# Second layer of a two-block network: three query columns side by side, and the memory written tile by tile behind them

## The reference, cut to what matters

```python
u = rms_norm(h, g_mix_pre[l])
u = sliding_window_sink_attention(u, positions, od_w_qkv[o], od_sinks[o], od_w_o[o])   # 16 heads, 4 kv heads
h = h + rms_norm(u, g_mix_post[l])
u = memory_cross_attention(rms_norm(h, g_x_pre[l]), mem, g_mem[l], w_xq[l], w_xkv[l], w_xo[l])
...
# inside memory_cross_attention: depends on mem alone, not on u
kv = (rms_norm(mem, g_mem) @ w_kv).reshape(B, M, 2, X_HEADS, X_HD)
```

## Time and profile before

| | us |
|---|---|
| median of three runs | 3557.65 (3555.43 to 3558.58) |
| the profiled execution | 3557.28 |
| its span in the trace | 3555.5, clock 0.972 |
| TensorE busy | 3385.7 (95%) |
| last pass over XH and XL in `swa` | ends 2888.94 |
| first pass of a memory unit | starts 2910.75 |

### The profile page before, as it was taken

The page is one execution under the profiler, slowest core; times in us unless marked ns, Lnnn a source line. Parts: engine busy times, 40 slices in busy tenths (PEclk is TensorE's granted clock), DMA queues, the critical chain, the costliest instruction groups (busy, mean ns, idle before and its releaser), DMA issues.

```text
span 3555.5 us, 38156 instructions
## 1 busy us (share of the span) xinstructions
PE 3385.7 (95%) x15620; PEld 2792.1 (79%) x15620; DVE 1782.2 (50%) x2721; ACT 1327.9 (37%) x2104; POOL 62.1 (2%) x64
## 2 busy tenths in 40 slices
PE   8999989999999999899999799999999889999998
PEld 6888767888878887778888678767888778768886
DVE  4333684433453337854334765546443664645444
ACT  3222554322232225543322544334322465434231
POOL 0000000000000000000000000000000000000000
PEclk9999999999999999999999899999999999999999
DMA  4333311333323332114333233212333313213332
GB/s 147 101 95 89 77 48 54 102 100 95 95 83 95 96 93 73 48 48 119 100 96 89 66 93 100 81 50 77 102 97 99 82 49 92 81 42 107 96 100 66
DMA packets 604287, 304.10 MB, mean 86 GB/s; under 512 B 43601, under 2 KB 601809, under 8 KB 603985
## 3 DMA queue, kind: packets, MB, share of 16 engines
q1 hardware_dynamic: 604112, 301.66, 29.7%
HBM read 299.52 MB, written 2.10 MB: 85 GB/s over the span
## 4 chain that ended last, share of the span: by engine, by line
PE 80%; DVE 11%; ACT 6%; DMA 1%; issue 1%; SPq 0%; DVEq 0%; ACTq 0%
PE ps L1592 25%; PE ps L1593 25%; PE ps L1600 25%; DVE wl L1979 2%; DVE Y L2152 1%; PE ps L1616 1%; PE ps L1609 1%; ACT wh L1764 1%; PE ps L1650 1%; PE ps L1749 1%; DVE XR L2075 1%; DVE tmp L1988 1%; ACT tmp L1833 1%; ACT XH L1806 1%; DVE XL L2061 1%
## 5 line engine op out<-in xcount | busy, mean ns | idle before, releaser
L1592 PE MATMUL ps<-XH,wh 128*128 128x512 f32 x2600 | 1050.7, 404 | 52.6 <-ACT XH L1806 14.6
L1600 PE MATMUL ps<-XL,wh 128*128 128x512 f32 (+1 forms) x2856 | 1067.9, 385 | 0.0
L1593 PE MATMUL ps<-XH,wl 128*128 128x512 f32 x2600 | 1027.6, 395 | 0.0
L1979 DVE TENSOR_TENSOR wl<-raw,wh 128x1024 fp32r<-128x1024 f32 (+1 forms) x565 | 680.2, 1209 | 530.8 <-ACT wh L1764 530.4
L1764 ACT ACTIVATE wh<-raw 128x1024 fp32r<-128x1024 f32 (+1 forms) x565 | 584.1, 1039 | 567.4 <-PE ps L1600 503.1
L1600 PEld LDWEIGHTS ps<-XL,wh 128*128 128x128 f32 x2856 | 545.9, 191 | 106.9
L1592 PEld LDWEIGHTS ps<-XH,wh 128*128 128x128 f32 x2600 | 498.8, 192 | 164.2 <-issue 36.1
L1593 PEld LDWEIGHTS ps<-XH,wl 128*128 128x128 f32 x2600 | 498.6, 192 | 104.7 <-issue 2.7
L1592 PE MATMUL ps<-HHa,wh 128*128 128x512 f32 x1088 | 427.7, 393 | 9.2 <-DVE HLa L1983 5.8
L1593 PE MATMUL ps<-HHa,wl 128*128 128x512 f32 x1088 | 423.6, 389 | 0.0
L1600 PE MATMUL ps<-HLa,wh 128*128 128x512 f32 x1088 | 407.9, 389 | 0.0
(11 more groups left out here) (310 smaller groups left out, 3056.1 us busy)
## 6 DMA issues: line engine op xcount, KB each, us to landing
raw<-in_ffn_w_gu SPq DMA_DIRECT2D x176, 512.0 KB, 3.8
raw<-in_w_ff SPq DMA_DIRECT2D x128, 512.0 KB, 4.1
raw<-in_ffn_w_down SPq DMA_DIRECT2D x64, 512.0 KB, 4.0
raw<-in_w_xkv SPq DMA_DIRECT2D x32, 512.0 KB, 3.9
raw<-in_ev_w_in SPq DMA_DIRECT2D x25, 512.0 KB, 3.9
raw<-in_ffn_w_down SPq DMA_DIRECT2D x32, 384.0 KB, 3.4
raw<-in_w_in SPq DMA_DIRECT2D x24, 512.0 KB, 3.8
raw<-in_w_out SPq DMA_DIRECT2D x64, 128.0 KB, 2.7
```

Of the source, the lines that this page charges most:

```text
L1592: e.matmul(bank[:, 0:n], t.wh[u % SPL][:, k, :], h, start=first, stop=False)
L1593: e.matmul(bank[:, 0:n], t.wl[u % SPL][:, k, :], h, start=False, stop=False)
L1600: m = e.matmul(bank[:, 0:n], t.wh[u % SPL][:, k, :], l, start=False, stop=last)
L1979: self.e.tensor_tensor(wl, raw, f32(wh), ALU.subtract).then_inc(self.s["lo"], self.tag("lo", f"lo.{i}"))
```

## The change

Two things. Query columns 5, 6 and 7 are now one group of three units, with the loop over `k` outside: each input tile is used by all three and is then done with. And tile `k` of the memory's halves is written after that: it waits for a new semaphore tag set by the last matmul on tile `k`, not for the last column. For this the halves of memory tile `k` lie in XL's tile `k`, side by side; before, the high halves lay in tiles 0 to 3 and the low halves in 4 to 7. The nine attention steps that stood among the parts are not called there any more, and the eight normalisations come in two lots of four, around query 4. The first layer keeps its order; only the places of its halves in XL change.

```diff
-    def project_group(self, cols, xs, k0=0, order=None):
+    def project_group(self, cols, xs, k0=0, order=None, each=None):
...
             self.p_first(us, k, n, n_k == 0, h, hi)
-            self.p_last(us, k, n, n_k == nk - 1, l, lo)
+            done = self.uid(f"x{k}.done") if each else None
+            self.p_last(us, k, n, n_k == nk - 1, l, lo, done)
             self.tick(n / T * len(us))
+            if each:
+                self.x_free[k] = f"mm.{us[-1][0]}" if n_k == nk - 1 else done
+                each()
...
+        def group(n, each):
+            got.extend(self.project_group(todo[len(got):len(got) + n], xs, each=each))
...
         def query(i):
             qb, qt = nxt()
-            self.x_used(qt)
...
-        for i in range(4, 8):
+        normed, parts = mem.normed(), mem.parts()
+        for _ in range(4):
+            next(normed)
+        query(4)
+        for _ in normed:
+            pass
+        nxt.group(3, lambda: next(parts))
+        for i in range(5, 8):
             query(i)
-            if i == 4:
-                for _ in mem.normed():
-                    pass
-        for _ in mem.parts():
-            next(self.filler[0], None)
+        for _ in parts:
+            pass
         for i in range(16):
             mem.unit(i)
...
-        self.mh = XL[:, 0:4, :].rearrange("p a (b t) -> p (a b) t", b=2)
-        self.ml = XL[:, 4:8, :].rearrange("p a (b t) -> p (a b) t", b=2)
+        self.mh, self.ml = XL[:, :, 0:256], XL[:, :, 256:512]
...
-                w.p_mem_hi(f"{self.k}.h{k}", self.mh[:, k, :], self.tile(k), (f"{self.k}.n{k}", w.x_free))
+                w.p_mem_hi(f"{self.k}.h{k}", self.mh[:, k, :], self.tile(k), (f"{self.k}.n{k}", w.x_free[k]))
...
+        if done and not last:
+            m.then_inc(self.s["mm"], self.tag("mm", done))
```

More of the change, by code:

```diff
@@ L417, in nxt @@
             return got.pop(0)
-        nxt.start, nxt.ahead = start, ahead
+        nxt.start, nxt.ahead, nxt.group = start, ahead, group
         return nxt
@@ L1593, in p_first, with p_last @@
             e.matmul(bank[:, 0:n], t.wl[u % SPL][:, k, :], h, start=False, stop=False)
-    def p_last(self, us, k, n, last, l, lo):
+    def p_last(self, us, k, n, last, l, lo, done=None):
         e, hold, at, t = self.e, self.hold, self.at, self.t
```

## The result

The changed kernel takes 3568.07 us, the median of seven runs (3565.31 to 3572.12), against 3557.65 for the kernel before: the ratio is 1.0034, 95% interval 1.0024 to 1.0044. It is 10.4 us **slower**, where 0.8 us faster was predicted and 3564 was the upper end of the range. The profiled execution took 3567.75 us, with a span of 3566.0. The page answers the earlier trace rows: TensorE has the same busy time, and one per cent more each of the chain that ended last lies on VectorE and on ScalarE.

A forecast was written before the change was run, and what follows sets the result against it. TensorE, busy 95% of the span, bounds the kernel; only pauses and low clock, 18.4 us, can be won. 2914.7 + 0.6 - 2911.1 - 3.0 - 0.4 = 0.8 us gained: 3556.9 us, range 3550 to 3564.

The forecast's parts named there:

- Normalisations and group: Query columns 4 to 7: pause of 3.51 us becomes 0.7; grouped passes and steps take 23.6 us without a pause.
- the price in front: Ahead of query 4's weights: the first four normalisations push TensorE later by 1.4 us.
- The clock that there was to win in the query columns: Query 5 to 7: 3.4 us lost to TensorE's low clock, all to be won.
- The burst: Behind the group: three rotations and three weight splits in a row hold TensorE, pauses of some 12 us against 9.2 before.
- T0: The end of the last query matmul, predicted at 2880.6 where it was 2888.9.
- The missing nine steps: Nine attention steps dropped ahead of the memory units cost 0.97 us each among memory passes, 8.7 to 9.0 in all.
- The row that I leaned on: Earlier trace, from the first memory pass to the output columns: TensorE busy 96.74 of 97.31 us at full clock.
- The drain: Nine leftover steps without scores, before the output columns' last two tiles: about 8 us, 3 exposed, plus 0.4 of clock.
- later pauses: TensorE's pauses behind the first memory pass in the kernel before: 0.6 us, counted as gained.
- the gain of 0.8: The whole forecast: 0.8 us faster than the kernel before.
- The rivals: Burst hidden: 3549, at best 3545, chance 0.10; drain dear: 3565, chance 0.10; memory halves late: 3559.4, chance 0.05.
- The clock in the drain: By the skill page, transposes and small products run at low clock: 5 us of work become 10, a 1 us loss.

The follow-up runs named there:

- b_norm44: The kernel before, with four of the eight normalisations written ahead of query 4's column and four behind it; 3556.13 us, ratio 1.0001.
- b_minus1: The kernel before with eight bare attention steps ahead of the memory units in place of nine; 3563.53 us, ratio 1.0018.
- a_nodebt: The changed kernel with the step count set to zero behind the group, so the first memory unit has two attention steps, not six; 3564.90 us, ratio 1.0024.
- a_plus9: The changed kernel with the nine bare attention steps put back ahead of the first memory unit; 3562.31 us, ratio 1.0016.
- a_plus1_nodebt: The changed kernel with one more attention step ahead of the memory units and the step count set to zero there; 3557.83 us, ratio 1.0005.
- c_one1: The changed kernel without the group: queries 5 and 6 as own columns, halves in query 7's column, one bare step; 3556.22 us, ratio 0.9998.
- b_bare1: The kernel before with normalisations four and four around query 4 and one bare attention step in place of nine; 3556.03 us, ratio 1.0003.
- c_one1_rate: As c_one1, with three attention steps in each of the first eight memory units in place of two; 3553.62 us, ratio 0.9992.
- a_rate9: The changed kernel with three attention steps in each of the first nine memory units in place of two; 3560.82 us, ratio 1.0011.

## Why the prediction was wrong

*Normalisations and group: right inside, the price in front partly by luck.* Predicted: the group from 2856.27 with 0.7 us of pause at full clock, the last query matmul done at 2880.6. Seen: 2856.45, 23.28 us of 23.81 busy, clock 1.00, done at 2880.26. The pause of 3.51 us became one of 0.53. But in front of the group, where 1.4 us were put, TensorE waited 1.21 us for a normalisation and then 1.52 for a head copy:

```profile
2851.76 0.44 PE L1655 MATMUL ps<-CT,tmp 128*128 128x128 f32 x2 [1.21 <-DVE tmp L2158]
...
2856.45 0.47 PE L1603 MATMUL ps<-XH,wh 128*128 128x512 f32 x1 [1.52 <-DVE HLa L1996]
```

The second isn't in b_norm44, and stands in the kernels with the group. It didn't show because the low clock took 1.5 us there and 3.1 in the kernel before, and the execution was 0.6 us ahead. The clock that there was to win in the query columns was also put too high, 3.4 us: that mean counts the pause, and over busy time it is 2.8.

*The burst: right.* Pauses of 1.4, 6.7, 2.2 and 1 to 2 us were predicted, 1.23, 6.80, 1.03 and 1.08 came, and the first unit ended at 2902.07 where 2902.1 stands. The last wait ended at T0 + 19.5, as predicted, though the clock had gone down (a mean of 0.77): the shorter pauses, 10.1 us where some 12 were put, and the slower work fill the same time. (0.6 of the agreement is luck: what lies ahead ran 0.6 us earlier in this execution.)

*The missing nine steps: the step that failed.* "Among memory passes they cost 0.97 each", and the sign to look for, "TensorE is busy all the time in the units behind". It was idle there for 6.2 us. I counted how many steps move and not against what they stand then. The row that I leaned on, 96.74 us busy of 97.31, holds for one alignment of two periodic streams, and b_minus1 shows that a single bare step fewer loses it.

*The drain: mis-sized.* Predicted 8 us with 3 of pause, and 0.4 of clock. It took 10.06 with 2.81 of pause; of the 7.25 busy, summed as in the table, the low clock took 1.7, and 5.5 are work, where I had 5. The low clock came within 1.4 us of the end of the pause of 2.78 us; in the drain of a_nodebt, behind one of 2.79 us at 3007.26, four value products still took 0.61 us, and the clock stayed at 1.00.

The sum then: from the end of the first unit to the last turn it took 19.9 us more than before (114.3 against 94.4), and 11.8 more were predicted (9.0 for the steps, 3.4 for the drain, less 0.6 of later pauses). Of these 8.1 the waits for head copies are 6.2, the drain's clock 1.3, and some 0.8 is work; the drain's pause was 0.2 shorter than put. With the 0.6 ahead, and less the gain of 0.8, that makes the 7.9 between pause and turn in the table. The last 3.2 us are behind the turn and were in nobody's sum: 2.9 of them are clock. Whether the change has a part in them is not shown, by one profile of each kernel; in b_minus1, a_nodebt and a_plus9 the stretch behind is within 1.2 us of the kernel before.

*The rivals.* None of them came. The drain took 10 us, not 13, and no low half was waited for (of the kernels with the group and early halves only the two without the debt wait for one, 5.1 and 6.8 us). The mechanism that did come is none of the three, and the debt, which stood in my description (at most one step at each call of `tick`, five steps in the first unit where there was one), was taken for a fact of the order and never priced: a_plus1_nodebt puts it at 5.4 us with the even alignment. So my burst was right as a time line and wrong as an unavoidable price.

*The clock in the drain.* In the drain of after the clock fell and came back while TensorE ran value products and transposes alone:

```profile
3006.04 0.71 PE L1663 MATMUL ps<-tmp,M 128*128 128x128 f32 x4 [2.78 <-ACT tmp L1859]
...
3007.44 1.22 PE L1663 MATMUL ps<-Y,M 128*128 128x128 f32 x4
...
3010.95 0.61 PE L1663 MATMUL ps<-M 128*128 128x128 f32 x4
```

Four value products take 1.22 us at the low level and 0.61 at the full one, and between these rows stand transposes and value products only. The Trainium skill, "TensorE: Matmul & The Clock Gate", Part 4 (PE-mode transpose), says that the full clock doesn't engage for transposes. In this mix it did, with a mean clock of 0.83 over the drain, as it had with scores in the mix at 2905.32; no run has transposes alone.

*What stays open.* Pairs of kernels that differ in nothing else show that the alignment costs (four pairs) and that the debt does (one pair, the even one); with both put right a_plus1_nodebt is 1.5 us above the kernel before, within the interval. That the order of weight split and head copy, on ScalarE and on VectorE, is why the alignment matters is read from traces; no kernel swapped these two. What is left between a_plus1_nodebt and c_one1 (1.6 us) is within the intervals.

## What to carry to other kernels

Where two periodic streams are woven together, a change that drops or adds items ahead of them also shifts the one against the other: try the shift by one by itself, in the kernel before, before you believe a sum of costs, and look what stands, on each engine, in front of the instruction that frees a buffer which the other stream needs. When columns are grouped, look what the weaving counter does with the group's larger strides: a debt that it pays back at once puts dependent work where nothing covers it. And what was waited for once in front of a bare handover is waited for again elsewhere: in b_bare1 eight bare steps less and a handover of 22 us less were worth nothing.

## What the runs showed of the hardware

The stretch behind the last turn has the same instructions in all kernels, and its idle time was 30.5 to 31.6 us in all twenty. What the low clock took of it was 5.6 us in the kernel before, 5.8 in b_minus1, 5.7 in c_one1_rate, 8.4 in after and 9.0 in a_rate9: after the same pauses TensorE worked at the low level for a longer or a shorter time. That alone is 3 us of a profiled execution. It is the same in front: the pause of 6.66 us ended anywhere from 2814.41 (c_one1_rate) to 2820.89 us (a_rate9), behind the same instructions in the same order. So two profiled executions of this kernel can't be compared by their spans below some 5 us; a stretch between two common events, with idle time and clock apart, can.
